# RWKV chunk scan on one core: Gram pair and transposes issued two steps ahead, old state added on DVE

## What is computed

```python
def step(state, inp):                       # state: (B, H, 64, 64), for each direction
    r_t, w_t, k_t, v_t, kk_t, a_t = inp
    sa = jnp.einsum('bhvk,bhk->bhv', state, -kk_t)
    state = (state * w_t[:, :, None, :]
             + sa[..., None] * (kk_t * a_t)[:, :, None, :]
             + v_t[..., None] * k_t[:, :, None, :])
    y = jnp.einsum('bhvk,bhk->bhv', state, r_t)
    return state, y
y_f, k_f = direction(xw_f, xa_f, 0, False)
y_b, k_b = direction(xw_b, xa_b, 1, True)
y = y_f + y_b
```

## Time and profile before

| | us |
|---|---|
| median of 3 timed runs | 1995.88 |
| lowest and highest of them | 1993.95, 1999.23 |
| the profiled execution | 1998.02 |
| its span, first to last instruction | 1996.1 |
| stretch of building rounds, layer 0 | 339 to 519.5 |
| plain round, layer 0 | 519.5 to 558 |

### The profile page before, as it was taken

The page is one execution under the profiler, slowest core; times in us unless marked ns, Lnnn a source line. Parts: engine busy times, 40 slices in busy tenths (PEclk is TensorE's granted clock), DMA queues, the critical chain, the costliest instruction groups (busy, mean ns, idle before and its releaser), DMA issues.

```text
span 1996.1 us, 27789 instructions
## 1 busy us (share of the span) xinstructions
PE 1706.4 (85%) x11192; PEld 1260.3 (63%) x11192; DVE 1076.7 (54%) x1533; ACT 729.3 (37%) x1160; POOL 291.3 (15%) x124
## 2 busy tenths in 40 slices
PE   2996855888887999999989988578878989999997
PEld 1783424656654888878858734266655768888785
DVE  6744557787344776772343243777763155454333
ACT  3433343445434223232243342435544232232322
POOL 0340000000011212121224400000000212121220
PEclk8998975788788999999989988668788989999999
DMA  6443110000032455542213210000001212323222
GB/s 275 169 158 111 43 58 1 1 2 2 1 137 95 168 192 187 189 169 84 88 48 113 93 51 1 0 2 2 2 2 43 85 63 84 105 84 105 85 87 82
DMA packets 34651, 162.96 MB, mean 82 GB/s; under 512 B 3840, under 2 KB 4096, under 8 KB 25856
## 3 DMA queue, kind: packets, MB, share of 16 engines
q1 hardware_dynamic: 34560, 161.65, 23.0%
HBM read 159.54 MB, written 2.10 MB: 81 GB/s over the span
## 4 chain that ended last, share of the span: by engine, by line
PE 72%; DVE 14%; ACT 7%; issue 5%; DMA 1%; POOL 0%; DVEq 0%; SPq 0%; ACTq 0%; POOLq 0%
PE bank L487 12%; PE bank L489 12%; PE bank L488 12%; PE bank_pair L487 4%; PE bank_pair L489 4%; PE bank_pair L488 4%; DVE work L1335 2%; PE bank L773 2%; PE bank_pair L577 2%; PE bank L774 2%; PE bank L548 1%; PE bank L556 1%; PE bank L751 1%; PE bank L703 1%; PE bank L789 1%
## 5 line engine op out<-in xcount | busy, mean ns | idle before, releaser
L487 PE MATMUL bank<-work_parts,y_mix_parts 128*128 128x512 f32 x792 | 315.8, 399 | 24.4 <-DVE work_parts L1498 16.2
L489 PE MATMUL bank<-work_parts 128*128 128x512 f32 x792 | 314.5, 397 | 0.0
L1511 DVE TENSOR_TENSOR work_parts<-work,y_mix_parts 128x1024 fp32r<-128x1024 f32 x66 | 169.2, 2564 | 253.2 <-ACT y_mix_parts L875 253.2
L1720 POOL TENSOR_TENSOR proj_weights_parts<-proj_weights,proj_weights_hi 128x1024 fp32r<-128x1024 f32 x54 | 130.9, 2427 | 1056.7 <-ACT proj_weights_hi L869 981.0
L1725 POOL TENSOR_TENSOR work_parts<-work,y_mix_parts 128x1024 fp32r<-128x1024 f32 x66 | 160.3, 2428 | 615.6 <-ACT y_mix_parts L875 615.6
L875 ACT ACTIVATE y_mix_parts<-work 128x1024 fp32r<-128x1024 f32 x132 | 132.9, 1055 | 250.9 <-DMA work<-mlp_dram 250.9
L488 PE MATMUL bank<-work_parts,y_mix_parts 128*128 128x512 f32 x528 | 208.8, 395 | 0.0
L487 PEld LDWEIGHTS bank<-work_parts,y_mix_parts 128*128 128x128 f32 x792 | 150.0, 189 | 66.4 <-issue 24.6
L489 PEld LDWEIGHTS bank<-work_parts 128*128 128x128 f32 x792 | 150.0, 189 | 35.5
L487 PE MATMUL bank<-work_parts,proj_weights_hi 128*128 128x512 f32 x304 | 126.3, 415 | 40.5 <-DVE work_parts L1498 25.9
L489 PE MATMUL bank<-work_parts,proj_weights_parts 128*128 128x512 f32 x304 | 123.8, 407 | 0.0
(11 more groups left out here) (253 smaller groups left out, 3150.4 us busy)
## 6 DMA issues: line engine op xcount, KB each, us to landing
work<-mlp_dram SPq DMA_DIRECT2D x66, 1024.0 KB, 4.8
work<-ada_dram SPq DMA_DIRECT2D x64, 512.0 KB, 4.6
proj_weights<-tiles_dram SPq DMA_DIRECT2D x57, 512.0 KB, 3.5
x_res<-ada_dram SPq DMA_DIRECT2D x24, 512.0 KB, 4.7
x_res<-x_dram SPq DMA_DIRECT2D x2, 2048.0 KB, 10.4
mixer_inputs<-ada_dram SPq DMA_DIRECT2D x8, 512.0 KB, 17.2
work<-mlaw_dram SPq DMA_DIRECT2D x4, 640.0 KB, 4.5
out_dram<-x_res SPq DMA_DIRECT2D x8, 256.0 KB, 2.2
```

Of the source, the lines that this page charges most:

```text
L487: mm(out, w_hi, x_hi, start=start, stop=False)
L489: return mm(out, w_lo, x_hi, start=False, stop=stop)
L1511: TTT(MW_L[q][:, 1], MW_IN[q][:, 1], plain(MW_H[q][:, 1]), ALU.subtract).then_inc(msp_v.sem, msp_v.one("l1"))
L1720: pool.tensor_tensor(ring_l[s], ring[s], plain(ring_h[s]), ALU.subtract).then_inc(spl_q.sem, spl_q.one(f"t{s}"))
```

## The change

Three things change in the scan, and nothing outside it.

1. The Gram products and the transposes are issued two chunks ahead instead of one. G and K of chunk 1 stand before step 0. In step s PE now runs R, L618, SA, G of chunk s+2, L of chunk s+1, S, Y, K of chunk s+2, and only then the building work.
2. The identity product L620 is gone. S writes only the chunk's contribution, and for s = 1 to 6 DVE adds the old SM to it (A, a new instruction) before it multiplies by the decay.
3. On ACT the copy T of the next chunk stands before the copy SA of this one. On DVE the mask of a chunk s > 1 waits for K of that chunk, which stands behind its G on PE.

```diff
-        sc_p = steps("sc_p", ["G0", "K0", "L0"] + [n for s in range(NCH) for n in ([f"R{s}"] if s else [])
-                     + ([f"G{s + 1}"] if s < NCH - 1 else []) + [f"SA{s}"]
-                     + ([f"K{s + 1}", f"S{s}", f"L{s + 1}"] if s < NCH - 1 else [])] + ["Y"])
+        sc_p = steps("sc_p", ["G0", "K0", "G1", "L0", "K1"] + [n for s in range(NCH) for n in ([f"R{s}"] if s else []) + [f"SA{s}"]
+                     + ([f"G{s + 2}"] if s < NCH - 2 else []) + ([f"L{s + 1}", f"S{s}"] if s < NCH - 1 else [])
+                     + ([f"K{s + 2}"] if s < NCH - 2 else [])] + ["Y"])
...
@@ scan_state on PE
-                if s < NCH - 1:
-                    mm(PS[1][:, 2 * P:3 * P], ident, cur.rearrange("p d v -> p (d v)"), start=True, stop=False, skip_group_check=True)
...
@@ rwkv_round on PE
+                    scan_gram(it, 1)
                     scan_values(it, 0)
+                    scan_tokens(it, cur, 1)
                 for s in range(NCH):
                     if scan:
                         if s:
                             scan_state(it, s)
+                        scan_solve(it, s)
+                        if s < NCH - 2:
+                            scan_gram(it, s + 2)
                         if s < NCH - 1:
-                            scan_gram(it, s + 1)
-                        scan_solve(it, s)
-                        if s < NCH - 1:
-                            scan_tokens(it, cur, s + 1)
+                            scan_values(it, s + 1)
+                        last = scan_update(it, s)
+                        if s < NCH - 2:
+                            scan_tokens(it, cur, s + 2)
                     if build and s in (0, 1):
                         rwkv_triangle(new, s)
...
-                    if scan:
-                        last = scan_update(it, s)
-                        if s < NCH - 1:
-                            scan_values(it, s + 1)
...
@@ scan_ring and scan_state on DVE
-                dve.wait_ge(sc_p.sem, sc_p.at(f"G{s}", it))
+                dve.wait_ge(sc_p.sem, sc_p.at(f"K{s}" if s > 1 else f"G{s}", it))
...
+                if s:
+                    own(sc_v, TTT(SM[(s + 1) % 2], grown, SM[s % 2], ALU.add), f"A{s}")
+                    dve.wait_ge(sc_v.sem, sc_v.at(f"A{s}", it))
+                    grown = SM[(s + 1) % 2]
```

More of the change, by code:

```diff
@@ L626, in scan_solve @@
                     rows = slice(64 * e, 64 * e + 64)
-                    last = mm(corner(PS[1], d, e), XT[it % 2][rows, d, s, :], RHS[rows, d, :], start=(s in (0, NCH - 1) and d == 0), stop=True,
-                              skip_group_check=True)
+                    last = mm(corner(PS[1], d, e), XT[it % 2][rows, d, s, :], RHS[rows, d, :], start=(d == 0), stop=True, skip_group_check=True)
                 own(sc_p, last, f"SA{s}")
```

7 lines of the change are left out of this document (4 added, 3 removed).

## The result

The changed kernel takes 2003.06 us (median of 15 runs, 1997.27 to 2008.72). The kernel before took 1995.88 us in 15 runs beside it. The ratio is **1.0043, interval 1.003 to 1.0056**: some 8.6 us slower, where 4 us faster was forecast. The profiled execution took 2005.25 us with a span of 2003.3.

What follows compares the result with a forecast made beforehand. PE's queue was taken to pace plain rounds, DVE the building rounds after step 1. Plain -6.4 plus building +3.8 gave -2.6 us; between that and a laid-out -5.4, -4 was taken: 1992 us, range 1984 to 2003.

Steps and rivals of the forecast that it cites:

- laid out in full: New order timed with trace durations for all rounds: plain rounds -3.9 and -3.5 us, building rounds -0.2 to +0.5 each, -5.4 in all.
- the hot step: Plain round, one step at the high clock: R to next R takes 3.40 us instead of 3.87, a gain of 0.47.
- step 3: Plain round: centring product, about 1 us, stands behind K on PE's queue and is no longer hidden; net change 0.
- step 5: Plain round: S, Y and K go ahead of the gate product that waits for ACT's logarithm; -0.75 us.
- step 6: Plain round: DVE's three normalisation operations hide beside the chain R, SA, S; step shrinks from 4.9 to 3.3 us, -1.6.
- the +0.9: Plain round, step 0: G of chunk 2 and L ahead of S, K ahead of R, at the low clock; +0.9 us.
- the price of 0.31 us: DVE's addition A makes the state ready 0.31 us later in 6 steps of every round.
- the keys' +1.2: Building rounds, step 1: DVE's second keys wait for ACT's factor, late because R waits behind PE's triangle; +1.2 us.
- rival (a): DVE keeps its pace in steps 0 and 1 of building rounds: 9 us more gained, 1983 us; chance with nearby outcomes 0.23.
- 2.1 us of DVE's waits: Building round with a tail: DVE waits of 0.46 and 0.73 ahead of masks, 0.89 ahead of step 5's state operation, come back.
- Rival (b): Clock rises later in each round because PE waits some 2 us for step 0's mask: +13.4 us, 2005; chance 0.18.
- The stated sign of error: Prediction is wrong if a building round moves by more than 1.5 us either way or plain rounds don't shrink.

Runs made afterwards that it cites:

- the run with this half alone: Kernel before with the new order and the addition in the plain rounds only, building rounds as before: ratio 0.996 to the kernel before.
- three pairs of runs: Addition against identity product back, in the changed kernel (1.0043, 0.9974), with PE's pauses filled (1.001, 0.9959), with the mask moved (0.999, 0.9932, building rounds only).
- the first pair: Changed kernel with the addition, ratio 1.0043, against the same new order with the identity product back in its place, 0.9974; both ratios to the kernel before.
- the second: Changed kernel with unread products filling PE's pauses, with the addition 1.001, against the same with the identity product back, 0.9959; ratios to the kernel before.

## Why the prediction was wrong

**Plain rounds: the mechanism was right, and the size within the noise.** Forecast -6.4 or, laid out in full, -7.4; the run with this half alone gave 8 us with an interval from 5 to 11, and its profile 8.3. The terms for one round were: the hot step 3.40, measured 3.28, because S starts 2.13 us after R instead of 2.24; step 3, forecast 0, measured -0.1; step 5, forecast -0.75, measured -1.0; step 6, forecast -1.6, measured -1.4. In the profiles step 0 changed by -0.2 in layer 0, where the clock rose after 1.4 us, and by +1.4 in layer 1, where it rose after 4.8; the +0.9 lies between. The plain round of layer 1 became 2.8 us shorter, near the forecast 3.2. That of layer 0 became 6.7 us shorter, and 2.8 of that is step 1 alone, which ran at the low clock before and at the high one after: 6.06 and 3.28, where -0.9 was forecast. There the low clock lasted 10.1 us into the round before and 1.4 us after; how much of that the order brought, the runs don't tell, and the gain of layer 0 is luck to that extent.

**The addition: the price of 0.31 us was right, its reach was not.** From its start to that of the decay are 0.30 to 0.32 us in the rows above, while an instruction that needs nothing of the decay started 0.21 after it (410.57 and 410.78 in the changed kernel). So the dependent pair of the earlier trace rows was the right row. By the Trainium skill, page "VectorE: DVE Perf Modes", section "The DRAIN you can't avoid", it would have been 0.21; the trace disagrees. In the old order it showed in two steps of a round, 2 x 0.31, and the timed runs show no cost of the exchange. In the new order taking it out gave 14, 10 and 11.6 us in three pairs of runs. The sum had 5 x 0.31 in each of four rounds, 6 us, beside the one in the state of step 1.

**Steps 0 to 2 of the building rounds: the waits were right, their size too high.** G does wait for the mask in step 0 (1.56 us), and R's copy does stand behind the triangle's. I had the state of step 1 late by 1.5 us, the keys' +1.2 and one addition; with the addition of step 2 and the 0.46 that come back there this makes some 1.4. Measured, step 0 took 1.9 us more, and steps 1 and 2 gave back 0.85 and 0.5: +0.5 together. The second keys start 9.37 us after the round's first copy of R where they started 9.00 after it, +0.4 and not +1.2. The difference is the triangle, put at 1.93 us of low clock: it took 1.10, since the clock had risen at 401.2. That is what rival (a) named, and its gain drowned in what follows.

**Steps 3 and 5: the failed step.** The sum of a building round had no term for PE's own work behind the new wait. I credited a round with 2.1 us of DVE's waits that would come back, and I treated bonus, centring, variance and gate as hidden beside DVE, as they were before, when no wait for the mask stood ahead of them: the bonus started 2.54 us after R. Now it starts 6.79 us after R. The mask ends at 418.47, and from there on PE has 6.8 us of work up to the next R, nearly all at the low clock. The price is there even with no fall: step 3 takes 7.12 to 7.15 instead of 6.67. The clock makes it 10.2. So steps 3 and 5 of this round grew by 3.5 and 2.1 us, where the sum had an addition of 0.31 in each and 0.89 back in step 5. I named the wait for the mask in step 0 and never looked for the same wait in the other steps, although DVE's order was known: in step 3 all of `inverse_8` up to row 6 stands ahead of the mask. DVE's waits did come back, and steps 4 and 6 became shorter by 1.0 and 2.4 us. The sum of a round with a tail was forecast at +0.95 and was +2.7 to +3.9; all building rounds together +3.8 and +13.6.

**The clock: the rival had the right resource and the wrong place.** Rival (b) gave 2005 by a clock that rises later at the start of each round. The time came out there, which is luck: in three of the four rounds with a tail the clock rose sooner after the round's start (1.4 to 1.6 us, before 4.0 to 4.7). Only the first two building rounds of layer 1 had it low for longer (7.8 and 6.4 us, before 4.9 and 5.1), and their step 0 took 9.36 and 8.75. What is new in the rounds with a tail are falls inside the round: 418.2 to 425.1 and 431.9 to 435.3, behind pauses of 1.98 and 1.52 us, and none there before. The first building rounds had such a fall before too (362.3 to 369.1, behind a pause of 2.26 us ahead of R), which could have warned me. The text expected PEclk to stay near 0.77 over all building rounds of layer 0 and it did (0.76 over 327 to 521), which was a bad thing to look at: a mean that takes in the parts between rounds hides a change of 0.95 to 0.85 inside one. The page "TensorE: Matmul & The Clock Gate" of the Trainium skill, section "What's actually happening", ties the low clock to an idle PE and the high one to a busy PE. The falls come in or right behind pauses, which is its direction; but PE was then busy 6.57 of 6.90 us at 0.51.

**The rest.** DVE's idle time ahead of the mask was expected under 15 us and is 28.7, of which the plain rounds alone have 24.0. The stated sign of error, a building round that moves by more than 1.5 us, came true. The measured 2003.06 lies just above the range of 1984 to 2003. Slower by more than 0.3% had been given a chance of 0.2.

**What stays open.** Why the addition costs 10 to 14 us in the new order is shown only in part. With the mask moved, the profile's building rounds give 6.0 us for it (236.3 to 230.3), the change in low clock included. In the other two pairs they give 10.2 and 14.0, and there falls of the clock became shorter or went away with the addition; the parts between the rounds add 3.4 in the first pair and take 3.2 off in the second. No run has the addition without its effect on the clock. Nor can I say why the clock fell behind a pause of 1.98 us in one round and not behind one of 1.74 in another. In the kernel before, PE paused for 1.83 us ahead of the gate product and for 2.09 ahead of R at 438.61, and the clock fell only at 440.8.

How the loss divides between queue and clock is known only for single steps, such as 7.15 and 10.2 for step 3. Every edit also moved the clock at the start of the rounds and between them, so no two runs differ by the queue alone.

## What to carry to other kernels

When a product is issued further ahead into the same buffer, ask who must first empty that buffer, how much work stands ahead of that on the other engine, and what now queues behind the wait; do it for every step of the loop and not for the first alone. A fix may be in the other engine's order: moving one copy on DVE was worth as much as any reordering of PE that was tried. When a wait is taken away, look at the clock behind the round too: the time that the engine saved may come back as one longer pause. If loops of one kernel have different bounds, give each its own order, since the same change was worth -8 us in the plain rounds and +16 in the building rounds.

## What the runs showed of the hardware

- A pause of 1.5 to 2 us on PE can be followed by several microseconds at the low clock with PE then nearly always busy. With the addition the same step took 10.2 us behind a pause and 7.15 with the pause filled; without it, 8.7 with a fall and 7.12 in the one round that had none. Useless products in the pauses made the kernel 6.6 us faster.
- The fall isn't tied to one pause. With two pauses filled it came in another of 1.26 us, in a step that had no such pause before. And a pause need not bring one: 1.74 and, in the kernel before, 1.83 us passed without.
- A fall can outlast the pause by far. Behind one pause of 3.36 us the low clock lasted 30.7 us, with PE busy 19.74 of 21.90 us in the part between two rounds.
- An exchange of one product for one addition that is worth nothing in one order (0.9996) is worth 10 to 14 us in another.
